# Expert outputs of a mixture of experts: stored in DRAM per job and gathered by adding DMAs, in place of a one-hot scatter in every job

## The reference

```python
logits = xt @ router                                  # xt: (256, 1024), router: (1024, 8)
top_vals, top_idx = lax.top_k(logits, 2)
top_w = jax.nn.softmax(top_vals, axis=-1)
gates = jnp.sum(jax.nn.one_hot(top_idx, 8) * top_w[..., None], axis=1)
for e in range(8):
    out = out + gates[:, e:e+1] * ((silu(xt @ wg[e]) * (xt @ wu[e])) @ wd[e])   # hidden width 3584
h = h + out ; return rmsnorm(h, final_norm)
```

## Time and profile before

| | us |
|---|---|
| median of 3 runs | 1539.51 (1538.94 to 1542.06) |
| the profiled execution | 1542.33 |
| its span, first to last instruction | 1540.5 |
| PE busy | 1512.3 |
| DVE busy | 1267.6 |
| ACT busy | 1009.5 |
| POOL busy | 7.2 |
| expert phase, from the first product of job 0 (563.94) to the end | 976.6 |

### The profile page before, as it was taken

How to read it: one execution, slowest core, us unless ns; L and a number is a source line. 1 busy time by engine, 2 the same in 40 slices (tenths; PEclk the granted TensorE clock), 3 DMA queues, 4 the chain that set the end, 5 groups by cost and what they waited for, 6 DMA issues and landing times.

```text
span 1540.5 us, 21674 instructions
## 1 busy us (share of the span) xinstructions
PE 1512.3 (98%) x7902; PEld 1265.5 (82%) x7902; DVE 1267.6 (82%) x1442; ACT 1009.5 (66%) x1154; POOL 7.2 (0%) x10
## 2 busy tenths in 40 slices
PE   7999999899999999999999999999999999999997
PEld 5888888699899678888888888888888888888885
DVE  3756666767875269999999999999999999999997
ACT  3444443743523147888887888887878888887886
POOL 0000000000000010000000000000000000000000
PEclk9999999999999999999999999999999999999999
DMA  9888443033004479999999999999999999999970
GB/s 360 311 284 282 164 165 109 1 123 123 1 1 166 178 264 396 397 384 361 387 361 364 383 358 366 387 359 358 385 381 348 379 380 347 378 380 347 376 287 27
DMA packets 203541, 439.36 MB, mean 285 GB/s; under 512 B 7265, under 2 KB 44641, under 8 KB 203362
## 3 DMA queue, kind: packets, MB, share of 16 engines
q1 hardware_dynamic: 200706, 434.05, 77.1%
q10 hardware_dynamic: 2208, 2.50, 0.5%
q0 software_dynamic: 576, 2.10, 0.4%
HBM read 427.09 MB, written 11.53 MB: 285 GB/s over the span
## 4 chain that ended last, share of the span: by engine, by line
PE 96%; DVE 2%; ACT 1%; issue 0%; DMA 0%; DVEq 0%; ACTq 0%
PE psum L1542 20%; PE psum L1544 20%; PE psum L1543 20%; PE psum L2339 5%; PE psum L597 5%; PE psum L2341 3%; PE psum L2263 2%; PE psum L890 2%; PE psum L2303 2%; PE psum L2305 2%; PE psum L2304 2%; PE psum L1560 2%; PE psum L2256 1%; PE psum L786 1%; PE psum L776 1%; PE psum L691 1%
## 5 line engine op out<-in xcount | busy, mean ns | idle before, releaser
L1742 DVE TENSOR_TENSOR w_lo<-ring,w_hi 128x1024 fp32r<-128x1024 f32 x672 | 804.6, 1221 | 50.7 <-ACT w_hi L1646 11.1
L1646 ACT ACTIVATE w_hi<-ring 128x1024 fp32r<-128x1024 f32 x672 | 711.4, 1062 | 185.3 <-PE psum L1544 185.2
L1542 PE MATMUL psum<-w_hi,xg_split 128*128 128x512 f32 x896 | 353.7, 395 | 0.3 <-DVE xg_split L1841 0.3
L1544 PE MATMUL psum<-w_lo,xg_split 128*128 128x512 f32 x896 | 349.4, 390 | 0.0
L1543 PE MATMUL psum<-w_hi,xg_split 128*128 128x512 f32 x896 | 348.7, 389 | 0.0
L1544 PEld LDWEIGHTS psum<-w_lo,xg_split 128*128 128x128 f32 x896 | 168.1, 188 | 35.7
L1542 PEld LDWEIGHTS psum<-w_hi,xg_split 128*128 128x128 f32 x896 | 168.3, 188 | 34.5 <-DVE w_lo L1742 0.7
L1543 PEld LDWEIGHTS psum<-w_hi,xg_split 128*128 128x128 f32 x896 | 168.4, 188 | 33.5
L1542 PE MATMUL psum<-w_hi,ht_split 128*128 128x512 f32 x448 | 176.1, 393 | 0.0
L1544 PE MATMUL psum<-w_lo,ht_split 128*128 128x512 f32 x448 | 174.6, 390 | 0.0
L1543 PE MATMUL psum<-w_hi,ht_split 128*128 128x512 f32 x448 | 174.3, 389 | 0.0
(11 more groups left out here) (367 smaller groups left out, 1587.8 us busy)
## 6 DMA issues: line engine op xcount, KB each, us to landing
ring<-o_moe_wg_dram SPq DMA_DIRECT2D x56, 2048.0 KB, 8.4
ring<-o_moe_wu_dram SPq DMA_DIRECT2D x56, 2048.0 KB, 8.8
ring<-o_moe_wd_dram SPq DMA_DIRECT2D x56, 2048.0 KB, 8.7
ring<-e_ffn_wg_dram SPq DMA_DIRECT2D x11, 1024.0 KB, 5.6
ring<-e_ffn_wu_dram SPq DMA_DIRECT2D x11, 1024.0 KB, 8.2
ring<-e_ffn_wd_dram SPq DMA_DIRECT2D x11, 1024.0 KB, 11.1
expert_rows<-work SPq DMA_DIRECT2D x1, 8192.0 KB, 29.4
ring<-e_w_in_dram SPq DMA_DIRECT2D x2, 2048.0 KB, 18.2
```

The lines of the kernel that those rows point to most:

```text
L1542: nc.tensor.matmul(dst, x_hi, hi, start=first, stop=False)
L1544: return nc.tensor.matmul(dst, x_hi, lo, start=False, stop=last_)
L1646: nc.scalar.activation(w_hi[:, (4 * i + n) % 4, :], piece(i, n), ACT.Copy).then_inc(m_hi, 1)
L1742: V.tensor_tensor(w_lo[:, r, :], piece(i, n), w_hi[:, r, :].bitcast(F32), ALU.subtract).then_inc(m_lo, 1)
```

## The change

Each job's gated output is stored as 128 rows of a second DRAM buffer of the same layout, and at the end the rows of each token are gathered and added into `h` by indirect DMAs. Only the last job's output still goes through the one-hot product.

- **PE**: the scatter (8 products) and the turning of the one-hot leave the loop. One turning stays, in job 0 at c = 5; one scatter stays, behind the loop. Ahead of the first down product of a loop job PE waits for ACT's two output copies.
- **ACT**: `outputs` writes plain gated rows to `y_rows` (a half of `xn`) and waits for the store of the job before and for the gate load; `outputs_split` (as before, into `Yhi`) is used for the last job.
- **DVE**: `outputs`, `scattered`, the one-hot, the gate sum and `PT` leave the loop; job 0 makes the plain one-hot of the last job. Ahead of job 0 the gate table `gt` and the first `Pg` are gone. The last adds to `h` wait for the gathers.
- **SP**: clears `gate_dram` in the first stage; behind the selector constants it copies the cleared `rows_dram` to `y_dram` (8 MB, DRAM to DRAM); per loop job it stores `y_rows` behind load 9 and loads 128 gates behind load 16. The rows of job 1 wait for eight scatters, not four.
- **POOL**: waits for the copy ahead of its row scatters; scatters the two gates of each token into `gate_dram` (four more indirect DMAs of one element a row); during the last job it gathers with adding from `y_dram` into `h`: two DMAs for the first choice, a wait, two for the second.

```diff
 # rwkv_sp
             sp.dma_start(pick, cst_dram[:, PICK_AT:PICK_AT + (B0 - 1) * P]).then_inc(pick_in, 16)
+            sp.dma_start(y_dram, rows_dram).then_inc(y_put, 16)
...
+        y_dram = nc.dram_tensor("expert_out", (2 * NE * P, D), F32).ap()
+        gate_dram = nc.dram_tensor("expert_gates", (2 * NE * P, 1), F32).ap()
+        y_put, g_in = sem("expert_out_written"), sem("expert_gates_in")
+        y_rows = xn[:, D:2 * D]
...
+            def gates(j):
+
+                at = sp.value_load(jobs[0:1, bass.ds(j, 1)], min_val=0, max_val=2 * NE - 1)
+                src = gate_dram.rearrange("(n p) o -> n p o", p=P)[bass.ds(at, 1), :, :]
+                sp.dma_start(gate, src.rearrange("n p o -> (n p) o")).then_inc(g_in, 16)
+
+            def out_block(j):
+
+                at = sp.value_load(jobs[0:1, bass.ds(j, 1)], min_val=0, max_val=2 * NE - 1)
+                dst = y_dram.rearrange("(n p) d -> n p d", p=P)[bass.ds(at, 1), :, :]
+                sp.dma_start(dst.rearrange("o p d -> (o p) d"), y_rows).then_inc(y_put, 16)
...
-                    sp.wait_ge(x_put, 64)
+                    sp.wait_ge(x_put, 128)
                     rows(0)
+                if i == 16:
+                    gates(0)
...
                     free(i - 7, j)
                     load(i, e)
+                    if i == 9:
+                        sp.wait_ge(m_yc, j * 2)
+                        out_block(j - 1)
                     if i == 14:
                         rows(j)
+                    if i == 16:
+                        gates(j)
 # moe_pe
-                    if c == 0 and not first:
-                        scattered(j)
-                    if c == 1:
-                        if not first:
-                            pe.wait_ge(s_h, j * 4 + 12)
-                        pe.wait_ge(m_pg, j + 1)
+                    if c == 5 and first:
+                        pe.wait_ge(m_pg, 1)
...
                     elif c >= 1:
+                        if c == 1 and not first:
+                            pe.wait_ge(m_yc, j * 2)
                         down(j, c - 1)
 # moe_act
             def outputs(j):
 
                 act.wait_ge(m_pc, j * NP)
+                act.wait_ge(y_put, j * 16)
+                act.wait_ge(g_in, j * 16)
+                for q in range(2):
+                    nc.scalar.activation(y_rows[:, 512 * q:512 * q + 512], psum[:, 4 + q, :], ACT.Copy,
+                                         scale=gate).then_inc(m_yc, 1)
 # moe_dve, ahead of job 0
-            V.tensor_tensor(oh1, oh1, wide("w1"), ALU.mult)
-            go(V.tensor_tensor(oh2, oh2, wide("w2"), ALU.mult))
-            V.tensor_tensor(gt[:, :, NE:2 * NE], oh1, oh2, ALU.add)
-            go(V.tensor_tensor(gt[:, :, 0:NE], oh1, oh2, ALU.add))
-            for b in range(TB):
-                last = V.tensor_scalar(Pg[:, b * P:(b + 1) * P], C("iota"), rk[:, b, 0:1], gt[:, b, 0:1], ALU.is_equal, ALU.mult)
-            last.then_inc(m_pg, 1)
 # moe_dve, in a job
-                    if i == 0 and not first:
-                        outputs(j)
-                    if (what, c) == ("u", 0) and not first:
-                        scattered(j)
...
-                    if (what, c) == ("d", 1):
-                        dve.wait_ge(m_pt, j + 1)
-                        V.tensor_reduce(gate, psum[:, 7, 0:256], AX.X, ALU.add)
+                    if (what, c) == ("d", 4) and first:
+                        dve.wait_ge(m_pt, 1)
                         V.tensor_scalar(PT[:, :], psum[:, 7, 0:256], 0.0, None, ALU.is_gt).then_inc(m_pte, 1)
-                    if (what, c) == ("d", 3):
-                        nxt = dve.value_load(jobs[0:1, bass.ds(j + 1, 1)], min_val=0, max_val=2 * NE - 1)
-                        onehot(nxt)
+                    if (what, c) == ("d", 3) and first:
+                        at = dve.value_load(jobs[0:1, 13:14], min_val=NE - 1, max_val=NE + 2)
+                        onehot(dve.value_load(jobs[0:1, bass.ds(at, 1)], min_val=0, max_val=2 * NE - 1))
 # moe_dve, scattered (behind the loop)
+                dve.wait_ge(x_put, 192)
 # moe_pool
-            pool.wait_ge(x_clear, 16)
+            pool.wait_ge(x_clear, 32)
             pool.wait_ge(x_at, 1)
+            pool.wait_ge(y_put, 16)
             pool.wait_ge(m_xg, 1)
...
+            pool.wait_ge(x_at, 2)
+            for i in range(2 * TB):
+                w = tb_[("w1", "w2")[i // TB]]
+                nc.gpsimd.indirect_dma_start(gate_dram, bass.IndirectOffsetOnAxis(row_at[:, i:i + 1], 0), w[:, i % TB:i % TB + 1],
+                                             None).then_inc(x_put, 16)
+
+            pool.wait_ge(r_jobs, 2)
+            last_job = pool.value_load(jobs[0:1, 13:14], min_val=NE - 1, max_val=NE + 2)
+            pool.wait_ge(y_put, last_job * 16 + 16)
+            nc.gpsimd.tensor_tensor(small[:, 502:504], tb_["w1"], tb_["w2"], ALU.add)
+            for i in range(2 * TB):
+                if i >= TB:
+                    pool.wait_ge(x_put, 128 + 16 * TB)
+                nc.gpsimd.indirect_dma_start(h[:, i % TB, :], None, y_dram, bass.IndirectOffsetOnAxis(row_at[:, i:i + 1], 0),
+                                             compute_op=ALU.add).then_inc(x_put, 16)
 # first stage, SP, behind the clearing of rows_dram
+                    sp.dma_start(gate_dram.rearrange("(p n) o -> p (n o)", p=P), zero_rows[:, 0:2 * NE]).then_inc(x_clear, 16)
```

More of the change, by code:

```diff
@@ L233, in trunk @@
         s_out = [sem(f"out{i}_written") for i in range(3)]
-        chain = {"dve": 0, "act": 0, "pool": 0}
-        CH = {"dve": dvc, "act": acc_, "pool": plc}
+        chain = {"dve": 0}
+        CH = {"dve": dvc}
         def link(eng, which, ins):
@@ L554, in rwkv_lora_sp @@
             sp.wait_ge(s_h, 4)
-            sp.wait_ge(x_clear, 16)
+            sp.wait_ge(x_clear, 32)
             one = lambda name: I[name].rearrange("a (k p) n -> p (a k) n", p=P)
@@ L1408, in trunk @@
         x_zero, x_clear, x_at, x_put, x_in = (sem(x) for x in (
-            "zero_rows_set", "expert_rows_cleared", "row_index", "rows_scattered", "expert_rows_in"))
+            "zero_rows_set", "expert_rows_cleared", "row_index", "expert_rows_moved", "expert_rows_in"))
+        y_dram = nc.dram_tensor("expert_out", (2 * NE * P, D), F32).ap()
+        gate_dram = nc.dram_tensor("expert_gates", (2 * NE * P, 1), F32).ap()
+        y_put, g_in = sem("expert_out_written"), sem("expert_gates_in")
+        y_rows = xn[:, D:2 * D]
         zero_rows = wu(5, 1024, 1024)
@@ L1581, in rows_turned, with scattered @@
                         last.then_inc(m_ga, 1)
-            def scattered(j):
-                pe.wait_ge(m_pte, j)
-                pe.wait_ge(m_yl, j * 2)
+            def scattered():
+                pe.wait_ge(m_pte, 1)
+                pe.wait_ge(m_yl, 2)
                 for b in range(TB):
@@ L1624, in moe_pe @@
                 job(j, False)
-            scattered(J)
+            scattered()
         def moe_act(act):
@@ L1662, in outputs, with outputs_split @@
                 act.wait_ge(m_pc, j * NP)
+                act.wait_ge(y_put, j * 16)
[3 more added lines that the diff above has]
+                                         scale=gate).then_inc(m_yc, 1)
+            def outputs_split(j):
+                act.wait_ge(m_pc, j * NP)
+                act.wait_ge(g_in, j * 16)
                 for q in range(2):
@@ L1693, in moe_act @@
             root_table()
-            outputs(J)
+            outputs_split(J)
             for b in range(TB):
                 for q in range(2):
-                    act.wait_ge(s_h, J * 4 + (9 + 2 * b + q))
+                    act.wait_ge(s_h, 13 + 2 * b + q)
                     n = 2 * b + q
@@ L1758, in moe_dve @@
             V.tensor_tensor(r3(tb_["d"], TB), mx[:, :, 1:2], mx[:, :, 0:1], ALU.subtract).then_inc(r_ex, 1)
-            gt, rk = r3(tb_["gt"], TB), r3(tb_["rk"], TB)
+            rk = r3(tb_["rk"], TB)
             dve.wait_ge(r_mm, 3)
@@ L1782, in moe_dve @@
             go(V.reciprocal(tb_["w1"], tb_["w2"]))
[L1783 to L1790 removed]
+            V.tensor_tensor(tb_["w2"], tb_["ex"], tb_["w1"], ALU.mult).then_inc(x_at, 1)
             A_, B_, O_ = tb_["ova"], tb_["ovb"], tb_["ovc"]
@@ L1832, in onehot @@
                     r_ = rk[:, b, bass.ds(col_, 1)]
-                    g_ = gt[:, b, bass.ds(col_, 1)]
-                    last = V.tensor_scalar(Pg[:, b * P:(b + 1) * P], C("iota"), r_, g_, ALU.is_equal, ALU.mult)
+                    last = V.tensor_scalar(Pg[:, b * P:(b + 1) * P], C("iota"), r_, None, ALU.is_equal)
                 last.then_inc(m_pg, 1)
@@ L1843, in gathered, with scattered, outputs @@
                 last.then_inc(m_xg, 1)
-            def scattered(j, o=0):
+            def scattered():
+                dve.wait_ge(x_put, 192)
                 for b in range(TB):
                     for q in range(2):
-                        dve.wait_ge(m_sc, j * 4 + (4 * o + 2 * b + q - 3))
```

(11 more changed lines are left out.)

2 lines of the change are left out of this document (removed).

## The result

The changed kernel takes **1524.2 us** (median of four runs, 1523.55 to 1528.12) against 1539.53 us (1538.94 to 1542.06), a ratio of 0.990 with a 95% interval of 0.9889 to 0.9912. Forecast were 1525.2 us, 14.3 less than before; measured are 15.3 less. In a second set of runs the same kernel took 1525.29 us (1524.3 to 1528.06) against 1539.56, 14.3 less.

A forecast was written before the change was run, and what follows sets the result against it. PE was taken to bound the expert phase. Seven loop jobs at 2.04 us less PE work gave 14.3 us, other terms 0 (boundary loss 0 to 3.5), so 1539.51 became 1525.2 us; range 1521 to 1530, chance 0.82.

The forecast's parts named there:

- The products out of PE: Loop jobs on PE: eight scatter products (1.82 us) and two one-hot transposes (0.22) go, 2.04 us a job, 14.3 in all.
- DVE is not the bound, so this is cover, worth nothing by itself: DVE in loop jobs: about 5.3 us less work, 109.0 us against a period of 118.6, counted as no gain.
- The boundary paragraph: Job boundary, PE without the scatter's 1.82 us: does it starve for split pieces? New stall 0 to 0.5 us a job.
- margin of 0.9 us: Job boundary: DVE ends the first piece at 688.0, PE wants it at 688.89; margin given as 0.9 to 1.3 us.
- SP's three new steps, the copy, the scatters, the gathers at 0: Store, gate load, register loads, 8 MB copy, gate scatters and adding gathers: all hidden beside other work, costing 0.
- The estimate of the room for the copy: Idle DMA stretch before the o_wo loads: the copy may last until about 494, 113 us, before it costs anything.
- DMA at 380 GB/s is enough, since 385 was seen: Loop jobs: 45.09 MB in 118.6 us needs 380 GB/s; job 0 moved 385 without ACT waiting, so cost 0.
- four short POOL issues with 17 us to spare: Gate scatters on POOL: 1.0 to 2.0 us each, landed by about 590, SP asks at 607.20; no cost.
- The lead of the ring: Weight loads are used some six loads, 34 us, after issue, so a delay of 1 to 3 us is hidden.
- The rival: Loop loads: DMA becomes the bound; gain gone at 373.7 GB/s, kernel 1560 us at 365; chance 0.06.
- The 358 GB/s of HBM: Skill page's HBM share: a job would take 126 us, kernel some 37 us more; set aside for traced 371 and 385.

## Why the prediction was right, and which step was not

- **The products out of PE** (forecast 2.04 us a job, 14.3 in all): shown. The period fell by 2.03 us, the eight products alone are worth 1.82, and the 0.2 left stand where the two transposes were.
- **"DVE is not the bound, so this is cover, worth nothing by itself"**: true only for DVE's part taken out alone (120.44 us with and without it), and wrong as a term of this sum, though the total was right. DVE's adds in one block, once PE's products are gone, cost 1.6 us a job. The boundary paragraph got its margin of 0.9 us (0.8 measured) only because DVE's outputs and adds were out as well. The sum rested on both removals, and the text priced one at nothing.
- **SP's three new steps, the copy, the scatters, the gathers at 0**: shown. The copy took 28.8 us, the lower end of the range given for it, not the 60 taken. The gathers' pair took 13 us inside 10 to 30. The estimate of the room for the copy stood up: copies that ended 14 us past it cost the kernel 12.
- **DMA at 380 GB/s is enough, since 385 was seen**: right in the outcome, with two things missed. The engines ran full for 280 us, with landings of up to 20.5 us, where the text had 13.4 at most and gave SP's steps "1 to 3 us" of delay; and the cause, the four byte writes, had been costed as four short POOL issues with 17 us to spare. The lead of the ring took it. The rival needed a limit under 374; the runs put it at 394 to 398.
- **The 358 GB/s of HBM.** The Trainium skill (DMA: Bandwidth & Descriptors, Where 436 GB/s comes from) has this figure as one of two cores' share of a memory stack, and says that it binds transfers between HBM and SBUF; by it a job takes 126 us. The periods of 118.6 us and the 394 to 398 GB/s disagree for this core, which runs alone, and the forecast was right not to go by it.
- **The 1 us beyond 14.3** is not settled as a cost of its own: the head of a run varies by up to 2.7 us with the clock around the router, and the second set gave 14.3.

## What to carry to other kernels

When two engines hand over at the same place, price the removal on each alone and on both: here work worth 1.8 us on one and 1.6 on the other cost 1.8 together, and taking out only one would have gained next to nothing. An engine with slack in its sum can still hold another when its other work comes in one block longer than the lead of the buffers between them. And count how many rows a DMA writes, not only its bytes: 512 single floats, 2 KB, took as much of the engines as 2.3 MB of loads.

## What the runs showed of the hardware that was not expected

- A copy of 8 MB from DRAM to DRAM landed in 28.8 us (291 GB/s), about as long as the store of zeros from SBUF (29.4 before, 28.0 after); of five in a row, the last four landed about 26 us apart (8.39 MB each, some 325 GB/s).
- The expert phase's loads with a few stores saturate at 394 to 398 GB/s on this core.
- Two adding gathers of 512 KB take 9.2 us with idle engines, beside the loads 13.2 us.
- TensorE's granted clock around the router fell to 0.50 in some executions and not in others. From the first router product to the first expert product the kernels took 21.65 us at a mean clock of 0.84 on that way, about 20.1 at 0.91 or 0.92, and 18.99 at 1.00, the kernel before and the changed one alike.
